# Recurrence of the RWKV layer: bonus products spread over two doubling levels, key blocks masked by twos, the decays' sums kept in two rooms

## What is computed

```
def step(state, inp):
    r_t, w_t, k_t, v_t, kk_t, a_t = inp
    sa = jnp.einsum('bhvk,bhk->bhv', state, -kk_t)
    state = (state * w_t[:, :, None, :]
             + sa[..., None] * (kk_t * a_t)[:, :, None, :]
             + v_t[..., None] * k_t[:, :, None, :])
    y = jnp.einsum('bhvk,bhk->bhv', state, r_t)
    return state, y
...
y = y + jnp.sum(rh * kh * r_k.astype(f32), axis=-1, keepdims=True) * vh
```

## Time and profile before

| | |
|---|---|
| median of 3 runs | 3028.71 us (3028.18 to 3035.36) |
| the profiled execution | 3027.78 us, of which its span is 3026.1 us |
| PE busy | 2840.3 us, 94% of the span |
| DVE, ACT, POOL busy | 1979.2, 1378.5, 1511.4 us |
| the recurrence, from the first product of pair 0's blocks to the end of pair 7's tail | 1717.2 to 2197.4 us of the span, 480.2 us |
| mean granted PE clock | 0.971 of full speed, 0.96 in the recurrence |

### The profile page before, as it was taken

How to read it: one execution, slowest core, us unless ns; L and a number is a source line. 1 busy time by engine, 2 the same in 40 slices (tenths; PEclk the granted TensorE clock), 3 DMA queues, 4 the chain that set the end, 5 groups by cost and what they waited for, 6 DMA issues and landing times.

```text
span 3026.1 us, 61868 instructions
## 1 busy us (share of the span) xinstructions
PE 2840.3 (94%) x25236; PEld 2248.9 (74%) x25236; DVE 1979.2 (65%) x2811; ACT 1378.5 (46%) x2298; POOL 1511.4 (50%) x1009
## 2 busy tenths in 40 slices
PE   8899999978999999999999999999888899999998
PEld 6544566856877878876688788888876688888887
DVE  6587895888787877786034255665546856665667
ACT  5475977134334333436333355455423434433445
POOL 0001000445776667764367346554364667767772
PEclk9799999989999999999999999999988999999999
DMA  9100000712222233221533212211131111112111
GB/s 316 43 1 15 2 2 2 250 42 75 84 92 83 69 94 100 83 85 56 195 117 120 99 46 67 82 60 53 36 100 30 56 42 56 57 41 66 45 56 70
DMA packets 194440, 225.98 MB, mean 75 GB/s; under 512 B 14863, under 2 KB 151650, under 8 KB 194210
## 3 DMA queue, kind: packets, MB, share of 16 engines
q1 hardware_dynamic: 182529, 180.66, 18.9%
q10 hardware_dynamic: 11680, 42.01, 3.8%
HBM read 185.15 MB, written 37.22 MB: 73 GB/s over the span
## 4 chain that ended last, share of the span: by engine, by line
PE 59%; DVE 10%; issue 10%; POOL 8%; ACT 3%; DMA 1%; SPq 0%; POOLq 0%; DVEq 0%; ACTq 0%
PE ps L148 13%; PE ps L149 13%; PE ps L150 13%; POOL w_lo L710 4%; PE ps L3707 3%; PE ps L3719 2%; PE ps L2226 1%; PE ps L2215 1%; PE ps L2237 1%; PE ps L3632 1%; POOL w_room L704 1%; DVE uc L1033 1%; PE ps L3756 1%; PE ps L3746 1%; DVE x_lo L998 1%
## 5 line engine op out<-in xcount | busy, mean ns | idle before, releaser
L148 PE MATMUL ps<-x_hi,w_hi 128*128 128x512 f32 x1232 | 494.7, 402 | 54.8 <-DVE x_lo L998 21.6
L149 PE MATMUL ps<-x_lo,w_hi 128*128 128x512 f32 x1232 | 486.7, 395 | 0.0
L150 PE MATMUL ps<-x_hi,w_lo 128*128 128x512 f32 x1232 | 486.6, 395 | 0.0
L710 POOL TENSOR_TENSOR w_lo<-w_room,w_hi 128x512 fp32r<-128x512 f32 x200 | 312.2, 1572 | 246.7 <-ACT w_hi L1178 246.4
L710 POOL TENSOR_TENSOR w_lo<-sq_room,w_hi 128x512 fp32r<-128x512 f32 x188 | 291.0, 1558 | 176.6 <-ACT w_hi L1178 176.4
L1033 DVE SCALAR_TENSOR_TENSOR uc<-u,pc,uc 128x1024 f32<-128x1024 f32 x176 | 329.1, 1880 | 24.1 <-ACT uc L1182 13.7
L148 PEld LDWEIGHTS ps<-x_hi,w_hi 128*128 128x128 f32 x1232 | 235.3, 191 | 127.4 <-issue 23.9
L1021 DVE TENSOR_TENSOR u<-u,ps 128x512 f32<-128x512 f32 x264 | 174.4, 683 | 188.8 <-PE ps L150 164.4
L150 PEld LDWEIGHTS ps<-x_hi,w_lo 128*128 128x128 f32 x1232 | 235.6, 191 | 50.5
L149 PEld LDWEIGHTS ps<-x_lo,w_hi 128*128 128x128 f32 x1232 | 236.1, 192 | 46.5
L148 PE MATMUL ps<-g_hi,w_hi 128*128 128x512 f32 x640 | 249.7, 390 | 0.6 <-DVE h L1099 0.5
(11 more groups left out here) (448 smaller groups left out, 6800.7 us busy)
## 6 DMA issues: line engine op xcount, KB each, us to landing
w_room<-in_f_w_up_dram SPq DMA_DIRECT2D x48, 512.0 KB, 5.0
rwkv_scratch<-rp_stage ACTq DMA_DIRECT2D x48, 512.0 KB, 3.5
sq_room<-in_f_w_up_dram SPq DMA_DIRECT2D x40, 512.0 KB, 4.9
ada_w<-in_ada_w_dram SPq DMA_DIRECT2D x80, 256.0 KB, 2.9
rc_raw<-rwkv_scratch SPq DMA_DIRECT2D x32, 512.0 KB, 3.8
d_ada_w<-in_ada_w_dram SPq DMA_DIRECT2D x24, 512.0 KB, 7.6
d_r<-in_ada_w_dram ACTq DMA_DIRECT2D x24, 512.0 KB, 5.7
sq_room<-in_f_w_down_dram SPq DMA_DIRECT2D x24, 512.0 KB, 4.3
```

The source lines that it names most:

```text
L148: pe.matmul(out, w_hi, x_hi, start=first, stop=False, skip_group_check=skip)
L149: pe.matmul(out, w_hi, x_lo, start=False, stop=False, skip_group_check=skip)
L150: return pe.matmul(out, w_lo, x_hi, start=False, stop=last, skip_group_check=skip)
L710: pool.tensor_tensor(slot_of(k.w_lo, s), src, slot_of(k.w_hi, s).bitcast(F32), ALU.subtract).then_inc(w_lo_done, 1)
```

## The change

It does six things in the recurrence, and moves one wait.

1. `bon_pe` is gone: the eight bonus products are issued one by one, behind each of the four groups of levels 2 and 3. DVE's copy of them moves from behind level 3 to behind level 4.
2. Blocks go by twos. The products of blocks x and x + 1 lie side by side in PSUM and DVE masks both with one operation of 512 elements a row (before: 256); the predicated copy is an operation of its own (`inverse_dve`). Because of this PE's order in the blocks is new.
3. The transposes are still one block at a time through bank 6, but at other places: that of block x + 1 (x even) is now the last thing in a round of two blocks, and that of x + 2 follows one chain step later.
4. The decays have two rooms each for input and sums (`w_ins`, `cums`), taken by turns.
5. So the scans for pair p + 2 move from the end of pair p's loop into its level 2 on DVE, one behind each of the two mask operations there, and SP's load of w for pair p + 2 goes up to the head of its loop. The second room of pair 1's w is memory that the projection stage uses, so that this load now waits for the stage's last product.
6. The first masks `first` are doubled for the predicated copy, and the small statistics `sm` live in another buffer (nothing else changes by it).
7. In pair 0 ACT waits for the projection stage's DMAs only after it has copied out block 4.

The core of the diff:

```
 def load_w(sp, q):
-    sp.wait_ge(sem["ar0"], q)
-    sp.dma_start(w_in, scr[W_, q, :, :]).then_inc(sem["w_ld"], 16)
+    if q >= 2:
+        sp.wait_ge(sem["ar0"], q - 1)
+        sp.wait_ge(sem["scan"], 2 * q)
+    sp.dma_start(w_ins[q % 2], scr[W_, q, :, :]).then_inc(sem["w_ld"], 16)
...
 def levels_pe(pe, p, lv):
+    bonus_lv = lv in BONUS_LV and p + 1 < PAIRS
...
             last.then_inc(sem["z_ps"][h], 1)
+            if bonus_lv:
+                bon_one(pe, p + 1, 4 * (lv - BONUS_LV[0]) + h)
...
                 l_last.then_inc(sem["l_ps"][h], 1)
+            if bonus_lv:
+                bon_one(pe, p + 1, 4 * (lv - BONUS_LV[0]) + 2 + h)
...
 def pe_all(pe):
-            for x in range(BLK):
+            for x in range(0, BLK, 2):
                 if p:
                     chain_pe(pe, p - 1, 2 * x)
-                key_pe(pe, p, x)
-                if x + 1 < BLK:
-                    removed_pe(pe, p, x + 1)
+                if x:
+                    transposes_pe(pe, p, x)
                 if p:
                     chain_pe(pe, p - 1, 2 * x + 1)
-                if x + 1 < BLK:
-                    transposes_pe(pe, p, x + 1)
+                for twin in range(2):
+                    key_pe(pe, p, x + twin)
+                if p:
+                    chain_pe(pe, p - 1, 2 * x + 2)
+                if x + 2 < BLK:
+                    for twin in range(2):
+                        removed_pe(pe, p, x + 2 + twin)
+                if p:
+                    chain_pe(pe, p - 1, 2 * x + 3)
+                transposes_pe(pe, p, x + 1)
...
             for lv in LV:
                 levels_pe(pe, p, lv)
-                if lv == 2 and p + 1 < PAIRS:
-                    bon_pe(pe, p + 1)
...
 def act_all(act):
     eye_act(act, slice(2, 3))
-    pair0.all_stored(act)
...
             for x in range(BLK):
                 copies_act(act, p, x)
+                if p == 0 and x == BLK // 2:
+                    pair0.all_stored(act)
...
 def dve_all(dve):
-            for x in range(BLK):
+            for x in range(0, BLK, 2):
                 removed_dve(dve, p, x)
                 if p:
                     state_dve(dve, p - 1, 2 * x)
+                inverse_dve(dve, p, x)
+                if p:
+                    state_dve(dve, p - 1, 2 * x + 1)
                 key_dve(dve, p, x)
                 if more and x == 4:
                     rkw_dve(dve, q)
...
                 if p:
-                    state_dve(dve, p - 1, 2 * x + 1)
+                    state_dve(dve, p - 1, 2 * x + 2)
+                    state_dve(dve, p - 1, 2 * x + 3)
...
+                    if p + 2 < PAIRS and lv == 2:
+                        scan_dve(dve, p + 2, s)
-                if more and lv == 3:
+                if more and lv == 4:
                     bon_dve(dve, q)
...
-            if p + 2 < PAIRS:
-                for i in range(2):
-                    scan_dve(dve, p + 2, i)
```

More of the change, by code:

```diff
@@ L3161, in rwkv_stage @@
     id64 = sb("id64", [P, C64])
-    first = sb("first", [P, 3, C64], U8)
+    first = sb("first", [P, 5, C64], U8)
     block = sb("block", [P, 4, C64])
@@ L3221, in pool_const @@
                 for c in range(2):
-                    done(pool.tensor_copy(first[hs(c), part, :], mask[hs(c), hs(c)]))
+                    for twin in range(2):
+                        done(pool.tensor_copy(first[hs(c), 2 * part + twin, :], mask[hs(c), hs(c)]))
             level(1, 1)
             for c in range(2):
-                done(pool.tensor_copy(first[hs(c), 2, :], mask[hs(c), hs(c)]))
+                done(pool.tensor_copy(first[hs(c), 4, :], mask[hs(c), hs(c)]))
         elif piece < CONST_PIECES:
@@ L3237, in rwkv_stage @@
     LV = range(1, 6)
+    BONUS_LV = (2, 3)
     STEPS = 2 * BLK
@@ L3246, in rwkv_stage @@
     raw = sb("raw", [P, 4, S])
-    r_in, k_in, w_in, a_in = (raw[:, i, :] for i in range(4))
+    r_in, k_in, w_even, a_in = (raw[:, i, :] for i in range(4))
     kk = sb("kk", [P, S])
@@ L3524, in receiving_key @@
         eng.wait_ge(sem["exp"], 3 * q + 3)
-        eng.tensor_tensor(ar[q % 2][:, :, 0, :], blocks(kk[:, :]), blocks(w_in), ALU.mult).then_inc(sem["ar0"], 1)
+        eng.tensor_tensor(ar[q % 2][:, :, 0, :], blocks(kk[:, :]), blocks(w_ins[q % 2]), ALU.mult).then_inc(sem["ar0"], 1)
     def removed_key(eng, q):
@@ L3644, in removed_pe @@
                 pe.wait_ge(sem["q_sb"], 4 * p)
+        elif twin == 0:
+            pe.wait_ge(sem["g2_sb"], BLK * p + x)
+        before_at, after_at = (slice((4 + 2 * i + twin) * C64, (5 + 2 * i + twin) * C64) for i in range(2))
         for c in range(2):
             for h in range(2):
-                pe.matmul(g[hs(c), h, 0:P].rearrange("p (i t) -> p i t", i=2), b_t[hs(h), toks(x, c)],
+                pe.matmul(g[hs(c), h, twin * P:twin * P + P].rearrange("p (i t) -> p i t", i=2), b_t[hs(h), toks(x, c)],
                           ar[u][hs(h), x, :, hs(c)], start=True, stop=True)
@@ L3654, in removed_pe @@
             for h in range(2):
-                last = pe.matmul(g[hs(1 - c), h, 3 * C64:4 * C64], b_t[hs(h), toks(x, c)], ar[u][hs(h), x, 0, hs(c)],
+                last = pe.matmul(g[hs(1 - c), h, after_at], b_t[hs(h), toks(x, c)], ar[u][hs(h), x, 0, hs(c)],
                                  start=True, stop=True)
@@ L3666, in key_pe @@
                 pe.wait_ge(sem["sx"], 2 * p)
+        elif twin == 0:
+            pe.wait_ge(sem["g3_sb"], (BLK * p + x) // 2)
         for c in range(2):
             for h in range(2):
-                pe.matmul(g[hs(c), h, 0:C64], ar[u][hs(h), x, 0, hs(c)], k_t[hs(h), toks(x, c)], start=True, stop=True)
+                pe.matmul(g[hs(c), h, twin * P:twin * P + C64], ar[u][hs(h), x, 0, hs(c)], k_t[hs(h), toks(x, c)],
+                          start=True, stop=True)
         for c in range(2):
             for h in range(2):
-                last = pe.matmul(g[hs(c), h, C64:P], k_t[hs(h), toks(x, c)], ar[u][hs(h), x, 1, hs(c)],
-                                 start=True, stop=True)
+                last = pe.matmul(g[hs(c), h, twin * P + C64:twin * P + P], k_t[hs(h), toks(x, c)],
+                                 ar[u][hs(h), x, 1, hs(c)], start=True, stop=True)
         last.then_inc(sem["g3_ps"], 1)
```

93 lines of the change are left out of this document (49 added, 44 removed).

## The result

The changed kernel takes **3051.67 us** (median of 7 runs, 3045.09 to 3063.4) against 3028.71 (7 runs, 3018.19 to 3035.36). The ratio is 1.0079, 95% interval 1.0063 to 1.0095: **+23 us**, outside my range, which ended at 3039. The profiled execution took 3048.84 us with a span of 3047.1; before, the span was 3026.1.

A forecast was written before the change was run, and what follows sets the result against it. PE, busy 94% of the span, was taken as the bound, so only its waits and slow clock could be won. Terms 8.4 + 3.4 + 0 - 10.9 - 2.7 + 1.8 = 0.0 gave 3028.5 us, range 3013 to 3039.

The forecast's parts named there:

- Blocks by twos, 19.4 us: Blocks of pairs 1 to 6: new PE waits give 19.4 us against 18.05 at full clock, +8.4 us in all.
- masks were the bound: Rival, faster: DVE's masks bound the blocks and the new PE waits don't bite, 3002 us; chance 0.08.
- half the waits: Rival, faster: half of the 4.6 us of new block waits goes, six pairs 14 us better, 3014 us; chance 0.14.
- Pair 7, +3.4: Level 1 of pair 7 waits for ACT's output copy, now ending 20.5 us after the pair's start: +3.4 us (2 to 4).
- Clock in blocks, -4.3: Four clock falls in blocks vanish with the 2.36 us wait for the first predicated copy: all 4.3 us come back.
- starts laid bare, +1.8: Block starts: PE's pauses at "issue", such as pair 3's 1.46 us, no longer hidden behind scans, count: +1.8 us (0 to +5).
- Levels, clock -6.6: Three clock falls in levels vanish, all 6.6 us come back; levels take 25.5 us at clock 1.00 in every pair.
- bonus 0: Levels 2 and 3: single bonus products cost 1.05 us more and fill about 1.0 of pauses: 0 (-0.7 to +0.7 a pair).
- Pair 0, -2.7: Start of pair 0: ACT's first copy, for which PE waited 4.6 us, starts 1.7 us earlier: -2.7 us (-4 to 0).
- clock falls elsewhere: Rival, slower: waits at the blocks' end drop the clock over sums and level 1, seven falls +11 us, 3040; chance 0.16.

The follow-up runs named there:

- twin at even addresses: The changed kernel with `first` of 7 rows, so that buffers behind it stand 256 bytes from where they were before the change: 3039.05 us, ratio 1.0037.
- the shift alone: The kernel before with one mask buffer 128 bytes a partition larger, so buffers behind it stand 128 bytes higher, no instruction changed: 3037.52 us, ratio 1.0028.
- spaced loads: The kernel before with two decay rooms, early scans and pair 0's edit; SyncE awaits the gate's and r's loads before issuing the next: 3020.07 us, 0.9978.
- rooms': The kernel before with only two decay rooms, scans moved to level 2 and pair 0's moved wait: 3024.43 us, ratio 0.9986.
- the run with small loads: Two decay rooms, early scans and pair 0's edit on the kernel before; k, v and gate loads cut to a sixteenth from pair 2: 3013.88 us, 0.9964.

## Why the prediction was wrong, step by step

The sum had no term for what cost most. By its own terms:

- **No term: addresses.** "The change adds and removes no product" was taken to mean that other stages stay as they are. They don't: +12.6 us between the changed kernel and its twin at even addresses, +9 us by the shift alone, and 9.2 us in the two projection stages themselves. Products inside the recurrence were not slower: in pair 4, at clock 1.00, PE was busy 15.93 us in the blocks and 23.84 in the levels of the changed kernel, 15.94 and 23.83 in its twin. That is some half of the 23 us.
- **Blocks by twos, 19.4 us: right in the sum, in part by luck.** At even addresses pair 1 took 20.04 us with a pause of 0.7 us in it, 19.3 without. But PE's own work is 15.7 us and not 14.8; the earlier trace rows had 15.6 already, and pair 7's waiting was 0.5 us by the trace, not 1.1. The waits were 3.5 us and not 4.6. Step 2 waited 0.9 us (1.1), the copies show 0.38 three times (the step from one pair of transposes to the next was 1.40 us, as laid out), step 15 0.7 (0.9), the sums 0.8. All waits bite, though a pause beside step 2 hid some of its wait in pairs 2 to 5; the rivals "masks were the bound" and "half the waits" fall.
- **Pair 7, +3.4:** +3.3 us in the changed kernel, +3.8 at even addresses. Right.
- **Clock in blocks, -4.3, and starts laid bare, +1.8: wrong, the failed step.** The clock's falls did stand behind the wait of 2.36 us, but I took them to be gone with it, and the pause for small. With that wait gone more of the program's pauses came into the open: 11.9 us in the six pairs' blocks of the changed kernel, 2.7 before. The clock fell with them in pairs 2 and 3. At even addresses blocks took 125.1 us in place of 6 x 19.4 = 116.4: 8.7 us against my 1.8, 6.9 us of error. Pauses of 7.2 us and two falls of the clock, some 2.5 us, are enough for it. The pauses grow where a transfer of the program meets the loads that SyncE issues at the same time, as spacing these shows; none of my rivals had the loads in it. Why a pause of 1.4 us near the start of pairs 3 and 5 stays with spaced loads is open; the store and the load of a were spaced in one run, and it still showed one of 1.26 us.
- **Levels, clock -6.6, bonus 0: the clock right, the bonus products not.** PE's busy time of a pair at clock 1.00 went from 22.7 to 23.0 us to 23.7 to 24.2, near the 1.05 more that I had put, and the falls are gone in nearly every pair. But the products filled less of the pauses than the 1.0 us that was to pay for them: at full clock PE idled 2.6 us of a pair's levels before, and 2.0 at even addresses. There six pairs took 156.1 us, 2.8 less than the 158.8 of before and not 6.6, so 3.8 us of error: 26.0 us a pair, not 25.5.
- **Pair 0, -2.7:** its blocks took 4.6 us less at even addresses, 4.0 in the changed kernel. PE's wait of 4.61 us became 1.53 and 0.75. Under-sized.
- **The rival "clock falls elsewhere"** had the right sign and a mechanism that came true in part. Behind the wait of 0.8 us the clock fell over the sums in pairs 1 and 6 of the changed kernel, 2.7 us together, and in one pair at even addresses, 1.4 us, where the rival had 11 for seven. The other falls came in the middle of the blocks, behind pauses.

With the predicted sum, 0, these give at even addresses 6.9 + 3.8 + 0.4 - 1.9 + 1.4 = +10.6 us; measured were +10.7 (3039.05 less the 3028.34 of the same set). That it fits so well is chance, since the terms come from one execution each and whole times of one kernel spread by up to 23 us.

## What to carry to other kernels

Before costing a change by its instructions, compare the buffers' addresses in both built kernels: here a mask table that grew by 128 bytes slowed products of other stages, and padding it to 256 cost nothing. A wait on an engine that is 94% busy may be cover for something that stands still anyway; take it away together with that (here: loads queued three deep in front of the program's own transfers), or it comes back under another name. Before moving a load, look at what its landing starts, and which small operation then runs beside it. Saving work on an engine that waits for the bound one was worth nothing here, and reordering the bound one to save it cost 19 to 24 us.

## What the runs showed of the hardware

- Back-to-back 128x512 products start 226.7 ns apart with the moving operand's buffer at 114272, 232.4 with it at 114400, and at 114528 again 226.7, with weights unmoved and the granted clock at 1.00 in each. Whether the operand's own address counts or its distance to the weights was not tried.
- Nearly all of PE's pauses at "issue" fall on multiples of about 127 products in every kernel, whatever these products are, and grow when loads of 512 KB lie in the queues: 9.5 us in six pairs with three issued together, 3.2 with two of them waiting for the last. The Trainium skill ("DMA: Bandwidth & Descriptors", Queues, rings and completion order) has each DMA engine take turns between its queues, a packet at a time; that agrees with the transfer that started 3.65 us behind PE's last place in place of 1.1, but no run here shows the turns.
- The clock fell in blocks behind long pauses in place of the wait, but not always: 0.83 to 0.92 in rooms' four pairs, 1.00 in the run with small loads around a pause of 2.46 us.
- DVE's 128x2 operation of 0.22 us took up to 2.08 us beside POOL's operations of 2.36 us. In eight profiled kernels it took over 0.6 us in blocks 17 times, and 16 times it ended 0.02 to 0.04 us after one of POOL's had ended.
